# Expert weights in a seventh set of buffers, and the routed rows of two experts gathered to the two halves of the partitions

## The reference, cut to what matters

```
yp = yp + mp                                   # mixers' output, through w_o
h = rmsnorm(yp, norm_ffn)
glog = h @ w_rg + b_rg;  g_idx = argmax(glog);  g_w = max(softmax(glog))
elog = h @ w_re + b_re                         # of the chosen group only
ev, ei = top_k(elog_sel, 2);  ew = softmax(ev)
combine = one_hot(8 * g_idx + ei) * g_w * ew   # 2 of 32 experts per token
a = h @ w_gate[e];  u = h @ w_up[e]            # 1024 x 256 each
yp = yp + (silu(a) * u * combine) @ w_down[e]  # 256 x 1024, summed over e
y = rmsnorm(yp, norm_final)
```

## Time and profile before

| | |
|---|---|
| median of 3 runs | 761.89 us (760.59 to 765.05) |
| the profiled execution | 762.18 us, of it span 760.4 us |
| mean granted TensorE clock | 0.945 |
| PE busy | 655.6 us (86%) |
| DVE busy | 306.8 us (40%) |
| ACT busy | 142.4 us (19%) |
| POOL busy | 139.0 us (18%) |
| bytes moved | 243.0 MB, mean 320 GB/s |
| the chain that ended last | PE 56%, DMA 25%, DVE 13% |

### The profile page before, as it was taken

How to read it: one execution, slowest core, us unless ns; L and a number is a source line. 1 busy time by engine, 2 the same in 40 slices (tenths; PEclk the granted TensorE clock), 3 DMA queues, 4 the chain that set the end, 5 groups by cost and what they waited for, 6 DMA issues and landing times.

```text
span 760.4 us, 13782 instructions
## 1 busy us (share of the span) xinstructions
PE 655.6 (86%) x5037; PEld 461.6 (61%) x5037; DVE 306.8 (40%) x1552; ACT 142.4 (19%) x406; POOL 139.0 (18%) x209
## 2 busy tenths in 40 slices
PE   5999999998999978999998999927897879667674
PEld 3888888677888856755432877626653445434331
DVE  3004987998868588610000121354324111111103
ACT  3122223233325322120010000120100101101013
POOL 0169964762000223200000000011000000000000
PEclk9999999999999999999999999957999898899997
DMA  9938989889988988977999989366999999999971
GB/s 309 260 127 281 312 271 401 288 279 342 360 292 281 392 273 287 382 275 275 390 409 386 297 320 409 140 256 239 361 394 401 348 382 401 402 400 402 416 285 59
DMA packets 94918, 243.00 MB, mean 320 GB/s; under 512 B 8850, under 2 KB 54546, under 8 KB 86530
## 3 DMA queue, kind: packets, MB, share of 16 engines
q1 hardware_dynamic: 57906, 192.99, 67.7%
q10 hardware_dynamic: 31328, 32.00, 12.7%
q0 software_dynamic: 5616, 17.11, 6.8%
HBM read 235.00 MB, written 9.11 MB: 321 GB/s over the span
## 4 chain that ended last, share of the span: by engine, by line
PE 56%; DMA 25%; DVE 13%; SPq 2%; issue 2%; ACT 1%; ACTq 0%; POOL 0%; DVEq 0%; POOLq 0%
PE zps L913 32%; DVE kall L1402 6%; PE nps L1087 5%; DMA ring_all<-in_w_up 5%; PE nps L1212 4%; DMA kall<-in_w_up 3%; DMA zret<-in_w_up 3%; DMA gain<-v_rows 3%; DMA qb<-in_w_down 3%; DMA ring_all<-in_w_ret_o 3%; PE zps L1235 3%; DMA out<-sfin 2%; PE nps L884 2%; DMA ring_all<-in_w_down 1%; SPq L444 1%
## 5 line engine op out<-in xcount | busy, mean ns | idle before, releaser
L913 PE MATMUL zps<-hT,ring_all 128*128 128x264 f32 x1152 | 274.8, 393 | 1.6 <-DVE hT L1583 1.0
L913 PEld LDWEIGHTS zps<-hT,ring_all 128*128 128x128 f32 x1152 | 217.4, 193 | 45.0 <-issue 5.3
L1402 DVE CUSTOM_DVE_ANT_0 kall<-kall,qb 128x128 f32<-128x128 f32 x512 | 153.0, 364 | 60.0 <-DMA kall<-in_cache_k 56.9
L620 POOL DMA_INDIRECT zatt<-h_rows,tidx_i x16 | 15.0, 939 | 349.4 <-DVEq L1671 194.4
L913 PE MATMUL zps<-headT,ring_all 128*128 128x264 f32 x256 | 58.5, 388 | 3.7 <-DMA ring_all<-in_w_ret_o 2.3
L913 PEld LDWEIGHTS zps<-headT,ring_all 128*128 128x128 f32 x256 | 48.1, 190 | 14.8 <-issue 4.8
L1087 PE MATMUL nps<-ring_all,zret 128*64 128x512 f32 x224 | 51.6, 599 | 2.8 <-DMA ring_all<-in_cache_v 2.8
L1745 DVE TENSOR_TENSOR qdT<-qdT,nps 128x64 f32<-128x64 f32 x32 | 7.1, 221 | 107.5 <-ACT qdT L825 107.0
L669 ACT ACTIVATE zt<-zps 128x264 f32<-128x264 f32 x56 | 21.8, 390 | 149.4 <-PE zps L913 148.0
L1212 PE MATMUL nps<-ring_all,zatt 128*32 128x128 f32 x768 | 30.0, 311 | 13.9 <-DMA ring_all<-in_w_up 12.4
L1570 DVE TENSOR_TENSOR hT<-zps,zatt 128x264 f32<-128x264 f32 x8 | 3.5, 433 | 93.1 <-PE zps L913 92.9
(11 more groups left out here) (364 smaller groups left out, 839.5 us busy)
## 6 DMA issues: line engine op xcount, KB each, us to landing
kall<-in_cache_k SPq DMA_DIRECT2D x64, 512.0 KB, 6.4
ring_all<-in_cache_v SPq DMA_DIRECT2D x56, 512.0 KB, 8.2
ring_all<-in_w_in ACTq DMA_DIRECT2D x26, 1024.0 KB, 8.8
ring_all<-in_w_gate SPq DMA_DIRECT2D x12, 1024.0 KB, 15.6
ring_all<-in_w_up SPq DMA_DIRECT2D x12, 1024.0 KB, 17.6
ring_all<-in_w_down SPq DMA_DIRECT2D x10, 1024.0 KB, 15.7
ring_all<-in_w_in SPq DMA_DIRECT2D x6, 1024.0 KB, 13.6
kall<-in_w_gate SPq DMA_DIRECT2D x5, 1024.0 KB, 22.8
```

What stands on the lines that cost most here:

```text
L620: pool.indirect_dma_start(out=rows, out_offset=None, in_=h2_rows, in_offset=bass.IndirectOffsetOnAxis(ap=col, axis=0), bounds_check=T - 1, ...
L913: mm = pe.matmul(zps[m % 2][:, 0:T], w[:, k, P * fb:P * (fb + 1)], rhs[:, k, :], start=(k == 0), stop=(k == KT - 1))
L1402: ins = v.tensor_tensor_reduce(kh, kh, qb[b % 2][:, P * h:P * (h + 1)], 1.0, 0.0, ALU.mult, ALU.add, scores[:, pg, AH * b + h:AH * b + h + 1])
```

## The change

SETS becomes 7. The seventh set lies in `zflat[:, 0:4096]` (the first two thirds of `zatt`) for gate and up, and in 2048 columns of the constants (`cst` from the causal mask on: masks, decays and rotary tables) for down. SP fills it ahead of the router: gate and up behind `down_in(0, 0)`, down behind `down_in(1, 1)`.

To make room, what lay in `zatt` moves. Two new buffers `rows_a` and `rows_b` (128 x 1024 each) take the place of `lgs`, `vnT`, `rtmp`, `rtmd`, `s1`, `sfin` and `qkd`, which become parts of them (`lgs` of `zt[0]`). `h2n` becomes `gain`, `rows_a`, `rows_b`. `xg[0]` is `rows_b` in partitions 0 to 63, `xg[1]` the same columns in partitions 64 to 127; `ysb` is `rows_a`, and `xgT` lies in `gain`. `x_tr` becomes 8 float32 matmuls with the identity at the tile position of the pair's half, in place of 8 transposes; three memsets on POOL clear the parts of `rows_b` that nothing has written. norm_final is loaded on SP's queue at the end, once all gate/up matmuls are over. ACT waits for the retention state's stores (`r_st`) before it goes on to the values. Two semaphores are merged into others.

```diff
-SETS = 6
+SETS = 7
-        lgs = sb("lgs", [G + NE, T])
+        rows_a, rows_b = sb("rows_a", [P, DM]), sb("rows_b", [P, DM])
+        lgs = zt[0][0:G + NE, :]
-        vnT = sb("vnT", [P, NB * AH])
+        vnT = rows_b[:, 584:584 + NB * AH]
-        rtmp = sb("rtmp", [P, 2, 2, P])
+        rtmp = rows_a[:, 0:512].rearrange("p (a b c) -> p a b c", a=2, b=2)
-        s1 = sb("s1", [P, RDV])
-        sfin = sb("sfin", [P, RDV])
+        s1, sfin = rows_a[:, 512:768], rows_a[:, 768:1024]
...
-        xg = [zflat[0:2 * CAP, DM * i:DM * (i + 1)] for i in range(2)]
-        ysb = zflat[:, 2 * DM:3 * DM]
+        xg = [rows_b[2 * CAP * i:2 * CAP * (i + 1), :] for i in range(2)]
+        ysb = rows_a
-        gate_up_w.append(headT[:, :, 0:2048])
+        gate_up_w += [headT[:, :, 0:2048], zflat[:, 0:4096].rearrange("p (a c) -> p a c", a=2)]
         down_w = [None, None, zflat[:, 4096:6144], hT[:, :, :].rearrange("p a b -> p (a b)")[:, 0:2048],
-                  scr[:, 0:2048], qb_all[:, :, :].rearrange("p a b -> p (a b)")]
+                  scr[:, 0:2048], qb_all[:, :, :].rearrange("p a b -> p (a b)"), cst[:, COL["causal"][0]:COL["causal"][0] + 2048]]
-        xgT = [zflat[:, 3 * DM + 512 * i:3 * DM + 512 * (i + 1)] for i in range(2)]
+        xgT = [gain[:, 512 * i:512 * (i + 1)] for i in range(2)]
-        h2n = zflat[:, 0:3 * DM].rearrange("p (t d) -> p t d", t=3)
+        h2n = (gain, rows_a, rows_b)
...
             down_in(0, 0)
+            gate_up_in(6, 6)
             sp.wait_ge(z_ready, 2 * (N_IN + 2 * N_O))
             gate_up_in(5, 5)
...
             down_in(1, 1)
+            down_in(6, 6)
             sp.wait_ge(z_ready, 2 * (N_IN + 3 * N_O))
             down_in(3, 3)
...
+            sp.wait_ge(e_GU, NE)
+            sp.dma_start(gain[:, :], norm_final.rearrange("(o d) -> o d", o=1).partition_broadcast(P)
+                         .rearrange("p o d -> p (o d)")).then_inc(fgain, 16)
...
+            for lo, hi in ((0, T), (328, 584), (648, DM)):
+                link(pool.memset(rows_b[:, lo:hi], 0.0))
...
-            act.dma_start(gain[:, :], norm_final.rearrange("(o d) -> o d", o=1).partition_broadcast(P)
-                          .rearrange("p o d -> p (o d)")).then_inc(fgain, 16)
+            act.wait_ge(r_st, 16 * RH)
...
                 for k in range(KT):
-                    mm = pe.transpose(zps[0][:, 2 * CAP * k:2 * CAP * k + rows], xg[par][0:rows, k:DM:KT], ident[0:rows, 0:rows])
+                    at = slice(2 * CAP * par, 2 * CAP * par + rows)
+                    mm = pe.matmul(zps[0][:, 2 * CAP * k:2 * CAP * k + rows], xg[par][0:rows, k:DM:KT], ident[at, at],
+                                   start=True, stop=True, tile_position=(2 * CAP * par, 0))
```

More of the change, by code:

```diff
@@ L212, in build @@
         scores = sb("scores", [P, NPG, NB * AH])
-        vnT = sb("vnT", [P, NB * AH])
+        vnT = rows_b[:, 584:584 + NB * AH]
         sn8 = sb("sn8", [NB, AH])
-        rtmp = sb("rtmp", [P, 2, 2, P])
-        rtmd = sb("rtmd", [32 + NB, 1, 2, P])
+        rtmp = rows_a[:, 0:512].rearrange("p (a b c) -> p a b c", a=2, b=2)
+        rtmd = rows_b[0:32 + NB, 328:584].rearrange("p (a b c) -> p a b c", a=1, b=2)
         scr = sb("scr", [P, 2304])
@@ L224, in build @@
         qdT = sb("qdT", [P, P])
-        s1 = sb("s1", [P, RDV])
-        sfin = sb("sfin", [P, RDV])
-        qkd = sb("qkd", [P, 2, RH * NB])
+        s1, sfin = rows_a[:, 512:768], rows_a[:, 768:1024]
+        qkd = rows_b[:, 264:328].rearrange("p (a b) -> p a b", a=2)
         ptab = sb("ptab", [1, NB * NPG], I32)
@@ L350, in build @@
             "y_square", "t_oh", "t_pos", "t_lhs", "t_idx", "t_e2"))
-        t_x, t_exp, t_tabs = map(sem, (
-            "t_x", "t_exp", "t_tabs"))
+        t_exp, t_tabs = map(sem, (
+            "t_exp", "t_tabs"))
         x_in2 = [sem(f"xg_in{i}") for i in range(2)]
@@ L362, in build @@
         fgain = sem("fgain")
-        h2_scaled = sem("h2_scaled")
         block = ctx.enter_context(nc.Block())
@@ L506, in _ @@
                         down_in(a, ex)
+                sp.wait_ge(e_GU, NE + XT)
+            sp.wait_ge(e_GU, NE)
+            sp.dma_start(gain[:, :], norm_final.rearrange("(o d) -> o d", o=1).partition_broadcast(P)
+                         .rearrange("p o d -> p (o d)")).then_inc(fgain, 16)
             for n, t in enumerate((0, 1)):
@@ L622, in gather @@
                                         bounds_check=T - 1, oob_is_err=False).then_inc(x_in2[par], 16)
-            def gather_for(p):
+            for p in range(NPAIR):
                 if p >= 2:
@@ L627, in gather_for @@
                 gather(p % 2, xg[p % 2], tidx_i[0:2 * CAP, p:p + 1])
[L629 to L632, removed]
             base = link_n[0]
@@ L808, in _ @@
                     for t in (0, 2):
-                        act.activation(h2n[0:ROWS[t], t, 0:768], xs[0:ROWS[t], t, 0:768], ACT.Square,
+                        act.activation(h2n[t][0:ROWS[t], 0:768], xs[0:ROWS[t], t, 0:768], ACT.Square,
                                        accum_out=st[0:ROWS[t], 6 + t:7 + t]).then_inc(y_sq, 1)
@@ L815, in _ @@
             for t, r in enumerate(ROWS):
-                act.activation(h2n[0:r, t, :], xs[0:r, t, :], ACT.Copy, scale=st[0:r, 9 + t:10 + t]).then_inc(h2_scaled, 1)
-                act.wait_ge(h2_scaled, t + 1)
-                act.dma_start(h2_rows[P * t:P * t + r, :], h2n[0:r, t, :]).then_inc(h2_out, 16)
+                link(act.activation(h2n[t][0:r, :], xs[0:r, t, :], ACT.Copy, scale=st[0:r, 9 + t:10 + t]))
+                act.dma_start(h2_rows[P * t:P * t + r, :], h2n[t][0:r, :]).then_inc(h2_out, 16)
             act.wait_ge(t_lhs, 1)
@@ L1182, in tile_base @@
             def tile_base():
-                pe.wait_ge(t_x, 1)
+                pe.wait_ge(t_lhs, 3)
                 pe.matmul(mps[:, 640:640 + NE], xcnt_b, upper[0:NE, 0:NE], start=True, stop=True)
@@ L1187, in tile_rows @@
             def tile_rows():
-                pe.wait_ge(t_lhs, 3)
+                pe.wait_ge(t_lhs, 4)
                 row_table(bps[:, 768:768 + XT], xA, xB)
@@ L1694, in tile_counts @@
                 link(v.tensor_copy(xcnt_b, xcnt.to_broadcast([NE, P])))
-                v.sem_inc(t_x, 1)
+                v.sem_inc(t_lhs, 1)
             def tile_tables():
```

## The result

The changed kernel is slower. Its median is 783.72 us (779.13 to 789.13), beside 761.5 us (760.59 to 765.05) for the kernel before; the ratio is 1.0285, 95% interval 1.0216 to 1.0353. The forecast was 756.7 us with a range to 761.5. The profiled execution of after took 786.23 us with a span of 784.4, to be compared with the 762.18 and 760.4 of before; 24.0 us more in the span.

What follows compares the result with a forecast made beforehand. The expert stage was bound by DMA transfers of weights: -8.0 (seventh set) + 2.5 (pair 0) + 1.2 (pairs 1 and 4) - 1.0 (hole at 605) = -5.3 us, giving 756.7 us, range 752.8 to 761.5.

Steps and rivals of the forecast that it cites:

- the price of a pair's 16 records: Turning a pair's x by identity matmuls: about 2.0 us at 2.4 GHz, 3.4 to 3.9 us at 1.2 GHz.
- rival C: Identity matmuls take four passes a transpose, not two: 3.9 us a pair, 767.5 us in all; chance 0.09.
- the term for pair 0: Pair 0's longer turn at the low clock, ahead of expert 0, delays the first refill and all transfers behind: +2.5 us.
- pairs 1 and 4: Their longer turns ahead of the first down refill: +0.95 us each, together +1.2 after 0.7 saved at expert 6.
- pairs 2 and 3: Their longer turns are covered by DVE's routing tables and a later reader: 0, or +1.9 us if uncovered.
- rival B: The start eats the gain: pairs 2 and 3 uncovered, hole at 605 stays, row writes late; 760.3 us, chance 0.18.
- Rival A: Clock returns during pair 0's longer work (-1.7) and the hole at 720 to 730 halves (-1.5): 753.7 us, chance 0.17.
- the eleven later pairs: Their longer turns, 10 us in all, fit into PE's 38 us of idle time in the full stretch: 0.
- the other buffer moves: Buffers moved to make room for the seventh set keep their instructions: put at nothing.
- worth its bytes: Seventh set fetched ahead of the router leaves 3.146 MB less to move at 392 GB/s: -8.0 us.
- The hole at 605 us: Dip in transfers at 605 to 610 us closes as expert 11's down weights land sooner: -1.0 us.
- norm_final's load and the memsets: The load at the end of SP's queue has 7 us of cover, POOL's memsets lie in idle time: nothing.

Runs made afterwards that it cites:

- e10: Seven sets, transposes and two state buffers, with routed rows rewritten so each transpose operand is contiguous: 754.18 us, against 751.92 us for the same kernel with strided operands.
- e3: The changed kernel, identity matmuls kept, with ACT writing the normalized rows so that each stationary operand is contiguous: 765.28 us.
- e1: The changed kernel with its identity matmuls put back to transposes, seven sets kept: 754.86 us.
- e6: The changed kernel with pairs 0 to 4 turned by transposes and pairs 5 to 15 by strided matmuls: 764.67 us.
- e7: The changed kernel with transposes put back and six sets of expert weights in place of seven: 766.92 us.
- e2: The kernel before, six sets and old buffers, with only its transposes made into strided identity matmuls: 787.69 us.
- e5: The changed kernel with pairs 0 to 4 turned by strided matmuls and pairs 5 to 15 by transposes: 775.83 us.

## Why the prediction was wrong

**The step that failed first is the price of a pair's 16 records.** The prediction put it at 2.0 us at 2.4 GHz and 3.4 to 3.9 at 1.2 GHz. Measured: 4.04 at a granted clock of 0.50 and 3.95 at 1.00 (16 records, 0.25 us each). The count of records was right. The rows it rested on the earlier trace rows had contiguous stationary operands, blocks of 128 neighbours in `cst` or `zret`; the turn's operand takes every eighth element. The transposes of before had the same step and took 1.1 us, and that was read as if the step were free; e10 shows that it was not, even there. e3 removes the step alone, and the prices of the prediction appear. It stood in the prediction as "I see no reason for another price". The bound of 3.9 us was there, but the range left it out with rival C.

**Second, what hides the pairs.** Even at the right price, the terms were too small. Between e1 and e3, F-G grew by 2.5 us, as the term for pair 0 says. D-F grew by 5.0 us: the prediction had +1.2 (1.9 for pairs 1 and 4 less 0.7 for expert 6), and 0 for pairs 2 and 3. The windows from F to D, in e1, e3 and after:

```profile
516.42:547.26 30.84, 26.57 (x531) 20.48 (x531) 14.21 (x61) 3.78 (x15) 3.73 (x4) 0.86 0.96 350
521.15:557.00 35.85, 33.46 (x563) 26.88 (x563) 14.31 (x61) 3.78 (x15) 3.72 (x4) 0.80 0.82 305
525.95:570.89 44.94, 43.05 (x563) 35.15 (x563) 14.39 (x61) 3.79 (x15) 3.74 (x4) 0.77 0.64 246
```

TensorE is busy for most of this stretch already in e1 (26.6 of 30.8 us). The turns of the four pairs in it took 4.3 us in e1, 8.4 in e3 and 16.1 in after. So in e3 they are 4.1 us longer, and TensorE's other work is 2.8 us longer at a lower granted clock (0.80 in place of 0.86); only 1.9 us of idle time gave way. In after the turns are 11.8 us longer, the other work 4.7, and 2.4 us of idle time gave way. All four pairs count, not two, and rival B's "pairs 2 and 3 are not covered" points the right way. D-F differs from one execution to the next as well, longer at a lower clock, so of the 5.0 us some may be chance. Rival A had the clock come back during pair 0's longer work, and it did not: expert 0's gate and up took 3.64 us in after as in before.

**Third, the eleven later pairs.** The prediction set 10 us against 38 us of idle time on TensorE and took 0. At the forecast's price that is right within the spread (L-D 186.0 in e3, 185.2 in e1). At 2.9 us a pair it is 32 us against 38 and is not: L-D grew by 6.7 us in e6 and 9.3 in after. That the idle time isn't spread as the pairs are is the likely reason; from 600 to 650 us e6 has less than 1 us of it.

**Fourth, "the other buffer moves".** They were put at nothing; e7 against before has them at 0.6% (0.3 to 0.9), some 5 us, and the cause stays open.

The whole of it by the dates, from e1 to after: G +6.6, of which the edit has no part; F-G +2.9; D-F +14.1; L-D +9.3; together 32.9, the difference of L. From before to after the seventh set stands against this: after's L-D is 2.6 us above before's, where e2, without the set, is 7.0 above.

**Rival C** had the right size at the high clock by luck, 3.9 us a pair from four passes a transpose. The records are two a transpose, each 0.25 us. Its +5.7 for pair 0 was too much (F-G +2.9), and its 767.5 us fell short by the other work in D-F and by the eleven later pairs. The Trainium skill, "TensorE: Matmul & The Clock Gate", section "Terms", names the transpose mode 4 times faster for float32. Here the trace agrees for the operand with the step, 3.95 us against 1.02 at a granted clock of 1.00 (3.9 times); without the step it is 1.93 against 0.64 (3.0 times). The prediction weighed that rule against contiguous rows and gave it 0.09.

**What held.** The seventh set is filled ahead of the router and is worth its bytes (e7 against e1). The hole at 605 us closed in e1 (share 1.01 to 1.03 in every 5 us from 590 to 615 us; e7, without the set, has 0.92 from 605 to 610). norm_final's load and the memsets are on no chain. All three signs of being wrong that the prediction named are in the trace of after: a pair at over 3 us at the high clock (3.95), transfers that run dry for over 4 us (563 to 568 us), and a last landing that comes no earlier (765.4 in place of 741.1 us).

## What to carry to other kernels

Take the price of a TensorE record from a row whose stationary operand has the same step between elements and the same mode, for two rows that agree in shape can differ by two (3.95 us against 1.93 for 16 records here). When an edit lengthens work between the start of a stage and the event that lets its transfers go, count every instruction in that queue at the clock granted there; transfers that start late into a full queue were not caught up here (L-D 184.7 us in e5, 185.2 in e1). Turn float32 blocks by transposes at either half of the partitions: seven sets with transposes took 754.9 us beside 763.9 for the kernel before, and 751.9 with two state buffers, where the further gain is not clear of the noise.

## What the runs showed of the hardware

A step of 32 bytes between the elements of a float32 stationary operand puts a floor under a record that the clock hardly moves, and it is another floor for matmuls (0.25 us a record) than for transposes (0.13 us). Time of a pair, from chains of the trace: the low clock is pair 0 at a granted 0.50 (e1, e10, after, e3), the high clock a later pair at 1.00 (e1 at 544.32 us, e10 at 546.16, after at 597.09, e3 at 553.16):

| | low clock | high clock |
|---|---|---|
| transposes (8 records), step of 8 elements | 1.13 us | 1.02 us |
| transposes, contiguous | 1.10 us | 0.64 us |
| matmuls (16 records), step of 8 elements | 4.04 us | 3.95 us |
| matmuls, contiguous | 3.66 us | 1.93 us |

At the low clock the step costs 3% for transposes and 10% for matmuls, at the high one 1.6 times for transposes and 2.0 times for matmuls. Which part of the load sets that floor no run tells.
